# A token's one-hot table for expert 0 split from that of experts 1 to 3, in the expert stage of a two-layer trunk step

## The reference

```python
t = h.reshape(B * T, Dm)
scores = sigmoid(t @ w_router)
# best: group with the highest sum of its two best; idx: the two experts in it; gate: their normalised weights
hg = einsum('nd,edf->nef', t, w_gate)
hu = einsum('nd,edf->nef', t, w_up)
y  = einsum('nef,efd->nd', silu(hg) * hu * gate[..., None], w_down)
```

## Time and profile before

| what | value |
|---|---|
| median of 3 executions | 1135.11 us (1132.82 to 1136.57) |
| profiled execution, span from first to last instruction | 1132.6 us |
| its own time beside the span | not recorded apart; the span lies 2.5 us under the median |
| TensorE busy, mean granted clock | 1065.7 us (94%), 0.979 of full |
| VectorE, ScalarE, GpSimd busy | 851.1, 689.5, 156.2 us |
| expert stage of layer 0, of layer 1 | from about 275 us, from about 811 us |

### The profile page before, as it was taken

How to read it: one execution, slowest core, us unless ns; L and a number is a source line. 1 busy time by engine, 2 the same in 40 slices (tenths; PEclk the granted TensorE clock), 3 DMA queues, 4 the chain that set the end, 5 groups by cost and what they waited for, 6 DMA issues and landing times.

```text
span 1132.6 us, 16007 instructions
## 1 busy us (share of the span) xinstructions
PE 1065.7 (94%) x5941; PEld 839.2 (74%) x5943; DVE 851.1 (75%) x1191; ACT 689.5 (61%) x867; POOL 156.2 (14%) x184
## 2 busy tenths in 40 slices
PE   6999998897999999999989998889799999999996
PEld 3798454693888888888869975468388888888886
DVE  4345556668899888898965546765889988888896
ACT  2423555544677777777724256654467777777764
POOL 0325200330011111111040011000101111111002
PEclk7999999998999999999999999999799999999999
DMA  9997889246999999999698371004599999999951
GB/s 351 344 338 214 322 292 288 92 141 263 370 356 373 370 381 370 372 376 376 229 377 251 135 241 74 1 1 155 220 386 372 366 378 382 374 371 369 367 200 58
DMA packets 82560, 319.86 MB, mean 282 GB/s; under 512 B 22464, under 2 KB 26926, under 8 KB 69692
## 3 DMA queue, kind: packets, MB, share of 16 engines
q1 hardware_dynamic: 67232, 285.58, 68.9%
q0 software_dynamic: 14160, 30.19, 7.9%
q10 hardware_dynamic: 1100, 3.23, 0.7%
HBM read 308.05 MB, written 30.57 MB: 299 GB/s over the span
## 4 chain that ended last, share of the span: by engine, by line
PE 81%; issue 7%; DVE 5%; ACT 4%; DMA 1%; POOL 0%; SPq 0%; DVEq 0%; ACTq 0%; POOLq 0%
PE bank L1209 16%; PE bank L1201 16%; PE bank L1202 16%; PE bank L891 3%; PE bank L917 3%; PE bank L921 3%; PE bank L914 3%; PE bank L1094 3%; PE bank L1260 2%; PE bank L1108 2%; ACT work L1603 2%; PE bank L986 2%; PE bank L1126 2%; PE bank L1027 1%; PE bank L1290 1%
## 5 line engine op out<-in xcount | busy, mean ns | idle before, releaser
L1663 ACT ACTIVATE work_r<-ring 128x4096 fp32r<-128x4096 f32 x93 | 338.1, 3636 | 120.0 <-PE bank L1202 108.6
L2244 DVE TENSOR_TENSOR ring_r<-ring,work_r 128x4096 fp32r<-128x4096 f32 x92 | 404.1, 4417 | 5.6 <-ACT work_r L1663 5.6
L1201 PE MATMUL bank<-work_r 128*128 128x512 f32 x768 | 305.2, 397 | 3.4 <-issue 3.1
L1202 PE MATMUL bank<-work_r 128*128 128x512 f32 x768 | 300.1, 391 | 0.0
L1209 PE MATMUL bank<-ring_r,work_r 128*128 128x512 f32 x768 | 193.8, 394 | 0.0
L1201 PEld LDWEIGHTS bank<-work_r 128*128 128x128 f32 x768 | 144.8, 188 | 33.9 <-issue 3.9
L1209 PEld LDWEIGHTS bank<-ring_r,work_r 128*128 128x128 f32 x768 | 143.7, 188 | 32.3
L1202 PEld LDWEIGHTS bank<-work_r 128*128 128x128 f32 x768 | 144.5, 188 | 28.7
L2507 POOL DMA_INDIRECT work<-hscr,idx x32 | 38.9, 1216 | 360.8 <-PE bank L1260 248.7
L1519 ACT ACTIVATE work_r<-ring 128x512 fp32r<-128x512 f32 (+1 forms) x48 | 28.8, 603 | 71.5 <-PE bank L921 71.5
L1943 DVE TENSOR_TENSOR ring_r<-ring,work_r 128x512 fp32r<-128x512 f32 (+1 forms) x48 | 32.1, 676 | 51.7 <-ACT work_r L1519 51.6
(11 more groups left out here) (270 smaller groups left out, 1546.5 us busy)
## 6 DMA issues: line engine op xcount, KB each, us to landing
ring<-in_w_gate SPq DMA_DIRECT2D x32, 2048.0 KB, 10.8
ring<-in_w_up SPq DMA_DIRECT2D x32, 2048.0 KB, 11.7
ring<-in_w_down SPq DMA_DIRECT2D x32, 2048.0 KB, 11.4
ring<-in_w_ada SPq DMA_DIRECT2D x24, 2048.0 KB, 9.9
ring<-in_w_in SPq DMA_DIRECT2D x4, 2048.0 KB, 15.8
yscr<-hT POOLq DMA_DIRECT2D x2, 3072.0 KB, 13.2
ring<-yscr SPq DMA_DIRECT2D x6, 1024.0 KB, 7.3
ring<-in_w_out SPq DMA_DIRECT2D x4, 1280.0 KB, 7.0
```

What stands on the lines that cost most here:

```text
L1201: mm(b[:], x_hi[:, k, :], hi[:, k, half, :], start=(k == 0), stop=False)
L1202: last = mm(b[:], x_lo[:, k, :], hi[:, k, half, :], start=False, stop=False)
L1663: A_(w_hi[:, slot % 2, :], ring[slot][:], ACT.Copy).then_inc(s_hi, 1)
L2244: tt(ring_r[slot][:], ring[slot][:], w_hi[:, slot % 2, :].bitcast(F32), ALU.subtract).then_inc(s_lo, 1)
```

## The change

The four sets of one-hot tables (one for each group of experts) become five. Set 0 is expert 0 alone: three operations 128 elements wide. Set 1 is experts 1 to 3: three operations 384 wide. Sets 2 to 4 are groups 1 to 3 as they were.

On VectorE the order is now: set 0; set 1's first operation; `slots(0)`; set 1's other two; in layer 1 the modulation read-out; `slots(1)`, which waits for `by_slot(1)`; then sets 2 to 4. On TensorE `by_slot(0)` is three products, and `by_slot(1)` (nine) stands behind A19 in layer 0 and behind the ten unread products in layer 1. The gather of expert 0 waits for set 0's `idx`, those of experts 1 to 3 for set 1's. The wait counts of the semaphores follow.

```diff
+SLOT_SETS = [(0, 0, 1), (0, 1, EPG)] + [(q, 0, EPG) for q in range(1, NG)]
+NSETS = len(SLOT_SETS)
...
-                    def by_slot(q):
-
-                        pe.wait_ge(s_oneh, n * NG + q + 1)
+                    def by_slot(i):
+
+                        q, first, end = SLOT_SETS[i]
+                        pe.wait_ge(s_oneh, n * NSETS + i + 1)
                         if q == NG - 1:
-                            pe.wait_ge(s_slot, n * NG + 1)
+                            pe.wait_ge(s_slot, n * NSETS + 2)
                         for t in range(NT):
-                            for e in range(EPG):
+                            for e in range(first, end):
                                 last = mm(bS[q][:, 4 * e:4 * e + 4], onehot[:, q, t, e, :], vals[:, t, q * EPG + e, 0:4],
...
                     by_slot(0)
                     if p == 0:
-                        for j in route[3]:
+                        for i, j in enumerate(route[3]):
                             ada(j)
+                            if i == 0:
+                                by_slot(1)
                         jobs_done((0, 1))
                     if p == 0 and not route[3]:
                         jobs_done(range(2, NB))
                         for _ in range(10):
                             mm(bG[:], onesb[:], swab[:], start=True, stop=True)
+                    if p or not route[3]:
+                        by_slot(1)
...
                     def slots_in_gate():
-                        by_slot(1)
                         by_slot(2)
+                        by_slot(3)
 
                     def slots_in_up():
-                        by_slot(3)
+                        by_slot(4)
                         weights_by_slot()
...
-                    def slots(q):
-
-                        v.wait_ge(s_slotp, NG * n + q + 1)
-                        pairs = bS[q][:, 0:4 * EPG].rearrange("p (e c b) -> p e c b", e=EPG, c=2)
-                        nc.vector.tensor_reduce(slotf[:, q], pairs, AX.X, ALU.add).then_inc(s_slotf, 1)
-                        v.wait_ge(s_slotf, NG * n + q + 1)
-                        ts(idx[:, EPG * q:EPG * (q + 1), :], slotf[:, q], BIG, None, ALU.add).then_inc(s_slot, 1)
+                    def slots(i):
+
+                        q, first, end = SLOT_SETS[i]
+                        v.wait_ge(s_slotp, NSETS * n + i + 1)
+                        pairs = bS[q][:, 4 * first:4 * end].rearrange("p (e c b) -> p e c b", e=end - first, c=2)
+                        nc.vector.tensor_reduce(slotf[:, q, first:end], pairs, AX.X, ALU.add).then_inc(s_slotf, 1)
+                        v.wait_ge(s_slotf, NSETS * n + i + 1)
+                        ts(idx[:, EPG * q + first:EPG * q + end, :], slotf[:, q, first:end], BIG, None, ALU.add).then_inc(s_slot, 1)
...
-                    def onehots(q):
-
-                        for t in range(NT):
-                            ins = tt(onehot[:, q, t], iotab[:].unsqueeze(1).to_broadcast([P, EPG, P]),
-                                     rk[:, t, q * EPG:(q + 1) * EPG].unsqueeze(2).to_broadcast([P, EPG, P]), ALU.is_equal)
-                        ins.then_inc(s_oneh, 1)
+                    def onehots(i, tiles=range(NT)):
+
+                        q, first, end = SLOT_SETS[i]
+                        for t in tiles:
+                            ins = tt(onehot[:, q, t, first:end], iotab[:].unsqueeze(1).to_broadcast([P, end - first, P]),
+                                     rk[:, t, q * EPG + first:q * EPG + end].unsqueeze(2).to_broadcast([P, end - first, P]),
+                                     ALU.is_equal)
+                            if t == NT - 1:
+                                ins.then_inc(s_oneh, 1)
...
                     onehots(0)
+                    onehots(1, range(1))
                     slots(0)
+                    onehots(1, range(1, NT))
                     if p == 0:
                         for j in route[2] if l else []:
                             ada(l, j)
+                    slots(1)
                     if p:
                         rest(0, 0, 0)
-                    for q in range(1, NG):
-                        onehots(q)
+                    for i in range(2, NSETS):
+                        onehots(i)
...
                     tokens_rest(1)
-                    slots(1)
                     slots(2)
+                    slots(3)
                     rest(1, 0, place(0, 0)[0])
-                    slots(3)
+                    slots(4)
...
-                            g.wait_ge(s_slot, NG * n + min((e + 2) // EPG, NG - 1) + 1)
+                            g.wait_ge(s_slot, NSETS * n + ((e + 2) // EPG + 1 if e + 2 else 0) + 1)
```

More of the change, by code:

```diff
@@ L2553, in count_passes_left @@
                     g.wait_ge(s_as, NE * done)
-                    for s, k in ((s_slotp, NG), (s_slotw, 1), (s_xt, NE), (s_hu, MOE_CH), (s_gd, NE), (s_gu, NE), (s_at, NE), (s_y, NE),
+                    for s, k in ((s_slotp, NSETS), (s_slotw, 1), (s_xt, NE), (s_hu, MOE_CH), (s_gd, NE), (s_gu, NE), (s_at, NE), (s_y, NE),
                                  (s_xhigh, 1), (s_xh, NE), (s_hi, MOE_CH), (s_sg, NE), (s_ah, NE), (s_ys, NE),
-                                 (s_rest, 2), (s_oneh, NG), (s_slotf, NG), (s_slot, NG), (s_gsl, 1), (s_gcol, NE), (s_xlow, 1),
+                                 (s_rest, 2), (s_oneh, NSETS), (s_slotf, NSETS), (s_slot, NSETS), (s_gsl, 1), (s_gcol, NE), (s_xlow, 1),
                                  (s_xs, NE), (s_lo, MOE_CH), (s_a, NE), (s_as, NE), (s_further, 1)):
```

## The result

The changed kernel takes 1143.6 us at the median (1142.6 to 1145.0, four runs), the kernel before 1134.9 us; the ratio is 1.0085 with a 95% interval of 1.0068 to 1.0103. It is slower by 8.7 us at the medians. Run again in another series, it was 1142.9 against 1134.0 us, 1.0081 (1.0066 to 1.0095).

The account below looks back on a forecast made before the run. TensorE was taken to set the pace from expert 0's gate product on, with no late start caught up. Stalls of 1.6 and 3.6 us plus clock losses of 1.6 and 1.6 gave +8.4 us: 1143.5 us, range 1138.0 to 1148.0.

Parts of the forecast that it names:

- What bounds: From expert 0's gate product to the stage's end, TensorE sets the pace; a start earlier by x is worth x.
- Narrower operations: VectorE's sets 0 and 1: six operations take 2.02 us in place of 1.81, 0.2 us dearer.
- The gather of expert 0: Ahead of the gate product: this gather is issued 1.4 us earlier in each layer.
- The cap: VectorE was ready only 0.88 and 0.86 us before L2260, so an earlier gather gives at most 1.7 us over both layers.
- The stall: VectorE waits at `slots(1)` for `by_slot(1)` behind TensorE's slow work; gate product later by 1.6 us (layer 0), 3.6 us (layer 1).
- The clock: TensorE, idle ahead of the gate product, falls to half clock: 1.6 us a layer, bounds nothing and 3.3 us each.
- The gather of expert 1: Now behind set 1 and two weight loads, it lands at 830.1 to 831.3 in layer 1, hidden barely: 0 us.
- Not slower: Rival: the earlier gather sets the gate product's start, if `by_slot(1)` is done before VectorE asks: -1.7 us, 1133.4 us; chance 0.05.
- The clock stays up: Rival: TensorE's clock does not fall, only the stalls count: +5.2 us, 1140.3 us; chance 0.13.

Follow-up runs that it names:

- early `by_slot(1)`: The changed kernel with `by_slot(1)` right behind `by_slot(0)`, ahead of the slow work in both layers: 1134.3 us, ratio 0.999 against the kernel before.
- TensorE kept busy: The changed kernel with more unread products on TensorE, six in layer 0 and seventeen in layer 1: 1141.5 us, ratio 1.0058 against the kernel before.
- layer 1 early: The changed kernel with `by_slot(1)` ahead of the ten unread products in layer 1 alone: 1135.5 us, ratio 1.0008 against the kernel before.
- layer 0 early: The changed kernel with `by_slot(1)` ahead of A19 in layer 0 alone: 1140.2 us, ratio 1.0059 against the kernel before.
- The experiment that issued it later: The changed kernel with `slots(1)` on VectorE behind sets 2 to 4 instead of ahead of them: 1144.5 us, ratio 1.0077 against the kernel before.
- three more on VectorE: The kernel before with three redundant 512-element one-hot operations at the end of the last set in each layer: 1138.1 us, ratio 1.0045.

## Why the prediction was right, step by step

- *What bounds.* That a late start is never caught up holds in all rows of the table.
- *Narrower operations.* Reckoned 0.20 us for 128 elements and 0.47 for 384; in the changed kernel they start 0.20 and 0.46 us apart. The Trainium skill, "VectorE: DVE Perf Modes", section on the TRN2 errata, names a fixed cost per instruction, and the estimate of 0.5 us a layer came from it. It was too dear for operations that follow each other without a wait; early `by_slot(1)` shows no loss from them. The 9.0 us that the prediction worked out from it was too high for another reason as well: VectorE waits 2.5 and 4.6 us behind these operations, and what they cost is for the most part lost in that wait.
- *The gather of expert 0.* 1.4 us earlier, as reckoned (3.73 to 2.31). The cap: 0.9 us were allowed in each layer; 0.8 and 1.0 came where nothing else stood in the way. The cap was set a little too low, because it took VectorE's time as given: in the kernel before VectorE waited 0.57 and 0.64 us at L2223 for `by_slot(0)`, and in the changed one it fills that wait with set 1's first operation.
- *The stall.* Reckoned 2.5 us and 4.6 us of idle VectorE, measured 2.57 and 4.56. In layer 1 the start was reckoned 3.6 us later and came 3.6 us later. In layer 0 it was 1.6 us by the stall alone; it came 1.8 us later with TensorE kept busy, but 2.8 and 2.6 us later in the changed kernel, where the six unread products ran at half clock and ended after VectorE was ready.
- *The clock.* 1.6 us a layer. Layer 1 measured just that, shown by filling the gap. Layer 0 is where the forecast is least exact: stall and clock were 3.2 us, and its four profiles say 4.6, 3.4, 3.0 and 0.9, by where the clock stood. The medians can't settle the split. Layer 0 costs 1.2 us by one pair of kernels (layer 1 early against both early) and 2.7 us by another (the changed kernel against layer 0 early), layer 1 costs 7.2 us (layer 0 early against both early) or 8.6 us (the changed kernel against layer 1 early), each uncertain by 2 us or more. So it is not shown whether the forecast was too high in layer 0 and too low in layer 1. That the sum came within 0.1 us of the median is luck: the parts were not known that well.
- *The gather of expert 1.* Reckoned as hidden, barely. It was hidden, with 11.2 us to land, and 2.9 us to spare in layer 1, since the lost clock delayed its turn as well. The experiment that issued it later met the wait.
- *The rivals.* "Not slower" was within 0.9 us of what the kernels with an early `by_slot(1)` did; its condition, that the products be done before VectorE asks, was the right one. "The clock stays up" describes the kernel with the gap filled, 1141.5 us where 1140.3 was given.

## What to carry to other kernels

Before an operation is split so that its first piece is ready sooner, look at what the result waits for next: here another engine was ready only 0.9 us ahead, and about that, not the 1.4 us won, was the most there was to win with its order as it stood. When a consumer of the second piece is put into an in-order queue, its place is set by the slowest thing ahead of its producer on the other engine; unread products that keep TensorE's clock up count as such work. Leaving TensorE idle for 4.0 us ahead of the gate product cost the late start here, and then 1.6 us more for products at the lower clock; with an idle time of 1.6 us (three more on VectorE) it was the late start alone.

## What was not expected of the hardware

The granted clock can stay low for long under a TensorE that is mostly busy: 0.50 from 272 to 289 us with 13.67 of 17.00 us busy. The same instructions of one layer cost 0.9 or 4.6 us by whether it comes up ahead of the gate product and stays up, a difference of some 40% of this change's whole effect. And the gather of expert 1 (its own rows, at most 128) depends on the loads beside it. Issued 1.8 to 2.8 us ahead of the first of two 2 MB loads, it landed in 3.8 to 5.5 us. Issued from 0.4 us ahead of that load to 2.6 us behind it, it took 10.4 to 12.0 us in every profile. Between these lie two cases, 1.0 and 1.1 us ahead, with 9.2 and 6.6 us. The Trainium skill, "DMA: Bandwidth & Descriptors", section on queues, rings and completion order, has the engines take turns between queues packet by packet; the trace agrees so far as the gather of layer 0 landed in 11.5 us and the second load beside it in 14.1, but that is not much earlier.
